# Gate and up projections by seven block products in more blocks, with merged joins, in a three-layer transformer kernel on one Trainium2 core

## The reference, cut to what matters

```python
D_FF = FFN_HIDDEN = 2816
# feed-forward of the first block (layer 0 of the kernel)
gate = jnp.einsum('bsd,df->bsf', h2, w_gate[layer])
up = jnp.einsum('bsd,df->bsf', h2, w_up[layer])
x = x + jnp.einsum('bsf,fd->bsd', jax.nn.silu(gate) * up, w_down[layer])

# feed-forward of the second block, twice (layers 1 and 2 of the kernel)
def conv_ffn(h, w_up, conv_w, conv_b, w_down):
    u = h @ w_up                                   # 1024 -> 2 * 2816
    c = lax.conv_general_dilated(u, conv_w[:, None, :], window_strides=(1,),
        padding=[(CONV_WIDTH - 1, 0)], ...) + conv_b   # 3 taps over the tokens, per channel
    g, val = jnp.split(c, 2, axis=-1)
    return (jax.nn.silu(g) * val) @ w_down
```

## Time and profile before

| | |
|---|---|
| median of 3 runs | 1713.58 us (1713.24 to 1714.19) |
| the profiled execution | 1712.91 us, its span 1711.1 us |
| PE busy in the span | 1700.8 us |
| DVE busy | 1278.1 us |
| ACT busy | 864.3 us |
| POOL busy | 361.6 us |

### The profile page before, as it was taken

One profiled execution on the slowest core, in us unless ns is written; L12 is line 12 of the kernel. 1 busy time (PEld: TensorE's weight loads), 2 busy tenths in 40 slices (PEclk: granted clock), 3 DMA queues, 4 the chain that ended last, 5 costly groups with the idle time before them and its releaser, 6 DMA issues.

```text
span 1711.1 us, 24883 instructions
## 1 busy us (share of the span) xinstructions
PE 1700.8 (99%) x9596; PEld 1476.2 (86%) x9596; DVE 1278.1 (75%) x1968; ACT 864.3 (51%) x1530; POOL 361.6 (21%) x264
## 2 busy tenths in 40 slices
PE   9999999999999999999999999999999999999998
PEld 8888888998998888888888988889898888898897
DVE  5789656897696846695979966755889687996575
ACT  5554533443354646554545533547877454454354
POOL 2003204442325011102144202022110213520200
PEclk9999999999999999999999999999999999999999
DMA  5212333334222221213233341323111234334122
GB/s 173 74 62 72 99 99 124 99 99 146 77 75 87 62 82 57 73 51 98 88 134 111 99 123 50 90 74 93 40 50 50 87 95 127 99 99 136 62 87 74
DMA packets 125196, 152.90 MB, mean 89 GB/s; under 512 B 7526, under 2 KB 96904, under 8 KB 125080
## 3 DMA queue, kind: packets, MB, share of 16 engines
q1 hardware_dynamic: 124776, 150.99, 27.9%
q10 hardware_dynamic: 304, 0.33, 0.1%
HBM read 148.61 MB, written 2.10 MB: 88 GB/s over the span
## 4 chain that ended last, share of the span: by engine, by line
PE 94%; DVE 4%; POOL 1%; issue 1%; ACT 1%; DVEq 0%; ACTq 0%; POOLq 0%
PE bk L2422 23%; PE bk L2424 23%; PE bk L2423 23%; PE bk L2464 5%; PE bk L2466 5%; PE bk L2465 5%; PE bk L2427 4%; PE bk L2569 2%; DVE FS L2624 1%; POOL FS L3011 1%; PE bk L2603 1%; PE bk L2530 1%; PE bk L2602 1%; DVE WL L2636 1%; PE bk L2557 1%
## 5 line engine op out<-in xcount | busy, mean ns | idle before, releaser
L2422 PE MATMUL bk<-R,WH 128*128 128x512 f32 (+1 forms) x1394 | 521.2, 374 | 0.9 <-DVE WL L2636 0.7
L2424 PE MATMUL bk<-R,WL 128*128 128x512 f32 (+1 forms) x1394 | 515.0, 369 | 0.0
L2423 PE MATMUL bk<-R,WH 128*128 128x512 f32 (+1 forms) x1394 | 514.8, 369 | 0.0
L2636 DVE TENSOR_TENSOR WL<-RAW,WH 128x1024 fp32r<-128x1024 f32 (+5 forms) x198 | 248.2, 1255 | 153.5 <-ACT WH L2861 152.3
L2861 ACT ACTIVATE WH<-RAW 128x1024 fp32r<-128x1024 f32 (+5 forms) x198 | 202.8, 1026 | 213.8 <-PE bk L2424 152.5
L2422 PEld LDWEIGHTS bk<-R,WH 128*128 128x128 f32 x1394 | 263.0, 189 | 45.3 <-DVE WL L2636 2.1
L2424 PEld LDWEIGHTS bk<-R,WL 128*128 128x128 f32 x1394 | 262.8, 189 | 44.9
L2423 PEld LDWEIGHTS bk<-R,WH 128*128 128x128 f32 x1394 | 263.2, 189 | 41.0
L3007 POOL TENSOR_TENSOR OVER<-TOK 128x1024 f32<-128x1024 f32 x28 | 76.3, 2725 | 382.0 <-DVE WL L2633 216.4
L2464 PE MATMUL bk<-WH,R 128*128 128x512 f32 (+4 forms) x394 | 144.7, 367 | 0.0
L2466 PE MATMUL bk<-WL,R 128*128 128x512 f32 (+4 forms) x394 | 139.3, 353 | 0.0
(11 more groups left out here) (235 smaller groups left out, 3251.8 us busy)
## 6 DMA issues: line engine op xcount, KB each, us to landing
RAW<-in_ffn_w_down_dram SPq DMA_DIRECT2D x44, 512.0 KB, 3.9
RAW<-in_ffn_w_up_dram SPq DMA_DIRECT2D x64, 256.0 KB, 3.0
TOK<-in_ffn_w_up_dram SPq DMA_DIRECT2D x14, 1024.0 KB, 5.1
RAW<-in_ffn_w_up_dram SPq DMA_DIRECT2D x28, 512.0 KB, 3.6
RAW<-in_w_down_dram SPq DMA_DIRECT2D x22, 512.0 KB, 3.6
RAW<-in_da_w_qkv_dram SPq DMA_DIRECT2D x32, 256.0 KB, 3.0
TOK<-in_w_gate_dram SPq DMA_DIRECT2D x7, 1024.0 KB, 5.4
TOK<-in_w_up_dram SPq DMA_DIRECT2D x7, 1024.0 KB, 5.0
```

The costliest lines, as they stand in the source:

```text
L2422: e.matmul(dst, lh, rh, start=start, stop=False)
L2423: e.matmul(dst, lh, rl, start=False, stop=False)
L2424: return e.matmul(dst, ll, rh, start=False, stop=stop)
L2636: e.tensor_tensor(low, sides(st.n, raw_home(st.n)), high.bitcast(F32), ALU.subtract).then_inc(on["wlo_dve"], 1)
```

## The change

- `SEVENS`: layers 1 and 2 use units for gate *and* up of blocks 4 to 10 (7 to 14 units each). Layer 0 adds block 3 (14 to 16 units), for which its parts become 3, 4 and 4 blocks (`BLOCKS`).
- The joins of a unit are four instructions instead of seven: two products that are joined alike share one bank (`o` is the column where a product begins), and a join takes both halves or writes both results. DVE does three of 512 columns and one of 256; ACT has one more copy. A unit holds five banks instead of seven.
- `Combined` takes two `FS` slots instead of four, with `PART` for the rest, gets a margin for free slots and another rank in the planner. Planning costs of `join` follow its width.

```diff
-PARTS = (range(0, 4), range(4, 8), range(8, 11))
-SEVENS = ({fb: (0, 2) for fb in range(4, 11)}, {fb: (0,) for fb in range(4, 11)}, {fb: (0,) for fb in range(4, 11)})
+THIRDS = (range(0, 4), range(4, 8), range(8, 11))
+BLOCKS = ((range(0, 3), range(3, 7), range(7, 11)), THIRDS, THIRDS)
+SEVENS = ({fb: (0, 2) for fb in range(3, 11)}, {fb: (0, 2) for fb in range(4, 11)}, {fb: (0, 2) for fb in range(4, 11)})
...
+EARLY = -2
+MARGIN = (3, 5, 5)
+RANKS = (1.5, 0.5)
...
-        if kind == "max":
+        if kind in ("max", "join"):
...
-                for kp in range(4):
-                    spawn(self.make(kp), 0.5)
+                N.uses += 4
+                self.makers = [spawn(self.make(kp), RANKS[0]) for kp in range(4)]
...
-                while kp and self.own[kp - 1] is None:
+                while kp and (self.own[kp - 1] is None or ("s4", kp - 1) not in self.of):
...
-                yield from N.use()
-                while len(fsl.fr) < 5:
-                    yield None
-                e, o, p, q = slots = [fsl.get() for _ in range(4)]
-                E, O, A, B = (FS[:, s.i, 0:S] for s in slots)
+                while N.spread is None:
+                    yield None
+                while len(fsl.fr) < self.margin:
+                    yield None
+                e, o = fsl.get(), fsl.get()
+                E, O = (FS[:, s.i, 0:S] for s in (e, o))
+                A, B = PART
...
-                    fsl.put(s, lo, w4.pool)
+                    if n < 2:
+                        fsl.put((e, o)[n], lo, w4.pool)
+                    else:
+                        part_free[n - 2] = [lo, w4.pool]
...
-            def product(n, half, name):
-                b = yield from bank("gemm")
-                st = yield step("piece", n=n, half=half, xs=X.operand(name), bank=b.i, after=counts([w_low[n].dve, X.ready, b.free]))
+            def product(n, half, name, b=None, o=0):
+                if b is None:
+                    b = yield from bank("gemm")
+                st = yield step("piece", n=n, half=half, xs=X.operand(name), bank=b.i, o=o, after=counts([w_low[n].dve, X.ready, b.free]))
                 if half or n == n2:
                     w_used[n] = st.pe
                 return b, st.pe
 
...
-            spawn(top_left(b, done), 0)
+            spawn(first(), 0)
+            b2, _ = yield from product(n1, 1, "a12")
...
-            b6, done6 = yield from product(n4, 0, "s2")
+            _, done6 = yield from product(n4, 0, "s2", b2, 256)
 
+                while q.first is None or len(fsl.fr) < 2:
+                    yield None
+                l, r = sorted((fsl.get(), fsl.get()), key=lambda s: s.i)
+                right = FS[:, r.i, 0:S]
+                st = yield step("join", dst=FS[:, l.i:r.i + 1:r.i - l.i, 0:256], src=halves_of(b2), x=one.unsqueeze(1).to_broadcast([P, 2, 256]),
+                                op=ALU.add, after=counts([done6, q.first, l.free, r.free]))
+                put_bank(b2, st.dve)
+                part_free[u % 2] = [st.dve]
+                third = yield step("join", dst=right[:, 256:S], src=BK[b7.i][:, 0:256], x=right[:, 0:256], op=ALU.add, after=counts([done7, st.dve]))
+                put_bank(b7, third.dve)
+                copied = yield step("keep", dst=FS[:, l.i, 256:S], src=right[:, 256:S], after=counts([third.dve, l.free]))
+                st = yield step("join", dst=right.rearrange("p (x c) -> p x c", x=2), src=BK[b5.i][:, 0:256].unsqueeze(1).to_broadcast([P, 2, 256]),
+                                x=right.rearrange("p (x c) -> p x c", x=2), op=ALU.subtract, after=counts([done5, third.dve, copied.act]))
+                put_bank(b5, st.dve)
+                q.low, q.both = [copied.act, st.dve], (l, r)
 
             spawn(middle(), 0)
...
+            b4, _ = yield from product(n4, 1, "a22")
+            _, done3 = yield from product(n2, 0, "s4", b4, 256)
+            X.over(done3)
+
+            def outer():
+                while q.both is None:
+                    yield None
+                l, r = q.both
+                at_l = FS[:, l.i, 256:S]
+                both = bass.AP(at_l.tensor, at_l.offset, [at_l.ap[0], [FW * (r.i - l.i) - 256, 2], [1, 256]])
+                st = yield step("join", dst=both, src=halves_of(b4), x=both, op=ALU.add, after=counts([done3, q.low]))
+                put_bank(b4, st.dve)
+                spawn(ev(0, l, st.dve), 0)
+                spawn(ev(1, r, st.dve), 0)
+
+            spawn(outer(), 0)
+
+        def halves_of(b):
+            return BK[b.i][:, :].rearrange("p (x c) -> p x c", x=2)
...
-                    if zone and part == 0 and fb == PARTS[0][-2]:
-                        held = Combined(N, counts(ptfree), counts(kfree[4 + 4 * NSK:]))
+                    if zone and part == 0 and fb == parts[0][EARLY]:
+                        part_free[0], part_free[1] = counts(tok_users), counts(tok_users)
+                        held = Combined(N, counts(ptfree), counts(kfree[4 + 4 * NSK:]), MARGIN[layer])
...
+                    for s in X.makers:
+                        s.rank = (RANKS[1], s.rank[1])
```

More of the change, by code:

```diff
@@ L502, in plan_ffn @@
                 zones[layer] = [len(chunks), len(chunks), len(units)]
-            for fb in PARTS[part]:
+            parts = BLOCKS[layer]
+            for fb in parts[part]:
                 sevenfold = SEVENS[layer].get(fb, ())
@@ L534, in build @@
         plan_rows(w_out, 512, 4)
-        for part in range(len(PARTS)):
+        for part in range(len(BLOCKS[0])):
             plan_ffn(part, ((w_gate, 0), (w_up, 0)), w_down)
@@ L546, in build @@
         plan_last_rows(da_o, 768)
-        for part in range(len(PARTS)):
+        for part in range(len(BLOCKS[1])):
             plan_ffn(part, ((up2[0], 0), (up2[0], 2816)), dn2[0])
@@ L1700, in seven @@
             q = Group()
-            q.first = q.second = q.third = q.left = q.right = q.y = None
-            one, two = PART[u % 2][:, 0:256], PART[u % 2][:, 256:S]
+            q.first = q.low = q.both = None
+            one = PART[u % 2][:, 0:256]
             def split(n):
@@ L1715, in product @@
                 return b, st.pe
-            def join(dst, b, done, x, op, *after):
-                st = yield step("join", dst=dst, bank=b.i, x=x, op=op, after=counts([done, *after]))
-                return st.dve
             while len(X.of) < 32:
@@ L1723, in seven, with first @@
             yield from split(n1)
-            b, done = yield from product(n1, 0, "a11")
-            def first(b, done):
-                st = yield step("keep", dst=one, bank=b.i, after=counts([done, part_free[u % 2]]))
-                put_bank(b, st.act)
+            b1, done1 = yield from product(n1, 0, "a11")
+            def first():
+                st = yield step("keep", dst=one, src=BK[b1.i][:, 0:256], after=counts([done1, part_free[u % 2]]))
+                put_bank(b1, st.act)
                 q.first = st.act
-            spawn(first(b, done), 0)
-            b, done = yield from product(n1, 1, "a12")
-            def top_left(b, done):
-                while q.first is None:
-                    yield None
-                s = yield from fslot()
-                q.top = yield from join(FS[:, s.i, 0:256], b, done, one, ALU.add, q.first, s.free)
-                put_bank(b, q.top)
-                q.left = s
-            spawn(top_left(b, done), 0)
+            spawn(first(), 0)
+            b2, _ = yield from product(n1, 1, "a12")
             yield from split(n3)
@@ L1764, in seven @@
-            spawn(middle(), 0)
-            b, done = yield from product(n4, 1, "a22")
-            def bottom_left(b, done):
-                while q.right is None:
-                    yield None
-                low = yield from join(FS[:, q.left.i, 256:S], b, done, one, ALU.add, q.third)
-                put_bank(b, low)
-                part_free[u % 2] = [low]
-                yield from ev(0, q.left, low)
-            spawn(bottom_left(b, done), 0)
-            yield from split(n2)
-            b, done = yield from product(n2, 0, "s4")
@@ L2864, in scalar_program @@
                         w.wait_ge(*done)
-                    e.activation(st.dst, BK[st.bank][:, 0:256], ACT.Copy).then_inc(on["keep_act"], 1)
+                    e.activation(st.dst, st.src, ACT.Copy).then_inc(on["keep_act"], 1)
                 elif k == "hi":
```

62 lines of the change are left out of this document (22 added, 40 removed).

## The result

| | before | after |
|---|---|---|
| median | 1713.88 us (1713.24 to 1714.27, 4 runs) | 1752.98 us (1751.67 to 1754.33, 4 runs) |
| the profiled execution, its span | 1712.91, 1711.1 us | 1751.67, 1749.9 us |

The ratio is 1.0231, with a 95% interval of 1.0218 to 1.0243: the kernel is 2.3% slower. The forecast of 1741 us had the direction and most of the size; the time lies in its range, 12 us above the number.

What follows compares the result with a forecast made beforehand. PE bounded the kernel before; with added taps and waits for POOL, DVE would bound layers 1 and 2: 2 x (10.3 + 3.3) + 2 = +29.2, less 1.7 in layer 0, +27.5, so 1741 us; range 1718 to 1766.

Steps and rivals of the forecast that it cites:

- The change of bound: In layers 1 and 2's parts with units, DVE's load instead of PE's work sets the length; chance 0.68.
- PE's waits: In layers 1 and 2, PE idles for low weights some 13 us per part of 8 units, 5 per part of 6.
- What POOL takes from DVE: DVE instructions with two SBUF operands wait for POOL's sums: 3.5 us per unit, read in layer 0.
- the turn: DVE's waits for POOL per unit above which the changed kernel is slower: about 2.3 us.
- Taps at 0.66 and joins at 0.60: DVE's start-to-start costs: 0.66 us per tap, also from SBUF, and 0.60 per join of 512 columns.
- The units' part of 94.2 us: Layers 1 and 2, part of 8 units (blocks 4 to 7): 94.2 us instead of 83.9, +10.3.
- The down projections at 0.5 us each (0 to 3): Down projections behind the parts with units in layers 1 and 2 begin late: 0.5 us per part, +2 for four.
- The parts of 6 units at 66.2 us: Layers 1 and 2, last part with units: 66.2 us instead of 62.9, +3.3.
- Layer 0 at -1.7 us: Block 3's added units save PE 1.7 us in layer 0; earlier combinations cost 0, bound 3.

Runs made afterwards that it cites:

- run with blocks 4, 8 and 9: The changed kernel, but in layers 1 and 2 up is a unit only in blocks 4, 8 and 9: 1718.41 us against 1713.5, ratio 1.0031.
- run with one filling matmul: The changed kernel with one more matmul of 256 columns before each product of a unit in layers 1 and 2: 1754.18 us against 1713.61, 1.0238.

## Why the prediction was right, and which terms were off

*The change of bound* held. DVE is busy for 99% of the parts of 8 units; PE waits there for low weights of `OVER` and `TOK`, and has no other cause of its waits inside them of any size. The runs without sums and with shortened taps show both halves of the reason: without POOL's sums the same change gains 10.7 us, without the taps it is at zero.

*PE's waits* were set at some 13 us in each part of 8 units and 5 in each of 6. They are 9.2 and 10.3, and 4.2 and 3.0: the rest of PE's lost time is in its slower matmuls, which count as busy.

*What POOL takes from DVE* held in size. From 925 to 1014 us DVE spends 20.3 us of 89 beyond the start-to-start times of its instructions, while POOL is busy for 36.1 us with the sums of six to seven units: 3.0 to 3.4 us per unit, where 3.5 were read in layer 0. The run without sums agrees: 97.25 - 72.96 = 24.3 us in 8 units, 3.0 each. The Trainium skill (SBUF — State Buffer, Who interferes with whom) calls the port pair that GpSimd and such a DVE instruction share an exclusive lock; the trace agrees for single instructions (3.12 instead of 1.21 us), but the cost per unit was not POOL's 5.4 us (2.42 + 2.98), since joins run beside a sum. The prediction sets the turn at about 2.3 us per unit; with its own terms it is 2.1 (27.5 over 20 units is 1.4 less than 3.5), which changes nothing here.

*Taps at 0.66 and joins at 0.60* held as start-to-start times: the four taps from SBUF at 1121.45 take 2.65 us until the next instruction starts, 0.66 each, and joined pairs of 512 columns take 0.68 us each, as forecast. A tap beside a sum takes 1.77 us (1008.68).

*The units' part of 94.2 us* was 1.2 and 1.6 us short. The sum lets the last weights decide, ready at 1008.75 in layer 1, and adds the last product: 1010.2, or 94.5 us after the start. But the chunk before them, ready at 1006.77, has 24 matmuls of its own to come first. With 36 x 0.120 that is 1011.1 at the full clock, or 95.4 us; in layer 2 it is 95.8.

*The down projections at 0.5 us each (0 to 3)* is the term that failed. "Their own weights stand a few instructions behind the last of the units'": those few are four taps and a join, 4.3 us, and PE needs the weights at once, while only the last block's activations can wait until the third quarter. From the 1011.1 at which PE could have been done it is 3.1 us to 1014.2, and 3.1 again in layer 2, in place of 0.5. (In layer 1 PE's lower clock hides 2 of them: its last product really ends at 1013.2.) In the parts of 6 units it is nothing, since the weights stand ahead of the taps there, ready at 1121.53, and PE's units end at 1124.4. Together with the term above, the parts of 8 units came out 9.0 us longer than 2 x 94.2.

*The parts of 6 units at 66.2 us* came out at 66.5 and 65.5. Some of that is luck: layer 1's holds 1.4 us of lower clock that the sum didn't have.

*The end of a layer* was left out of the sum: the stretch from the last unit to the end of the span is 45.6 us instead of 42.7, with a wait of 1.61 us for the last result. 2.9 us. The run with blocks 4, 8 and 9 shows that this can be 7 us.

*Layer 0 at -1.7 us* was half right: the first unit of layer 1 begins 0.5 us earlier. The units of block 3 start with a wait of 0.68 us for a combination (288.84 us), which was set at zero with a bound of 3. By itself the layer's change, with the merged joins, is worth -1.0 us, within 0.2%.

*The clock* wasn't in the prediction at all. It costs 1.3 to 2.5 us after a long wait, but in the parts of 8 units the kernel doesn't pay it, since DVE sets their end. The part of 6 units of layer 1 gets longer by it: the last 36 matmuls, from 1118.65, take 5.75 us to 1124.40 instead of 36 x 0.120 = 4.3, so 1.4 us. The layer doesn't, as far as the run with one filling matmul shows, which lost at `R` what it gained there.

The span: -0.5 to the first unit of layer 1, +14.6 and +15.0 in the parts of 8 units, +3.6 and +2.6 in those of 6, +0.4 in their down projections, +0.3 from there to layer 2, +2.9 at the end make 38.9 of 38.8 measured; 27.5 were forecast. Against the forecast that is 9.0 - 2.0 us for the parts of 8 units with the down projections, 2.9 for the end and 1.2 for layer 0; the rest is small.

## What to carry to other kernels

When PE is busy for 99% and the next engine for 75%, look in each stretch at how long before PE's need the other engine's last operand is ready. In layer 0's part of 8 units, which the changed parts came to resemble, that slack was 0.2 us, and the work added to DVE came out almost in full: 28 taps x 0.66 = 18.5 us, less 1.3 for the joins, made 98.5 us of 81.0. Count an engine's instructions at what they take beside the neighbour that holds them up, not at their price when it is quiet. When a piece is moved ahead in a queue, look at everything it now stands in front of: the low weights gained 1.4 us where they were late and lost 0.88 where they weren't. And replacing fewer gemms (5 units in 4 blocks and 4 in 3) kept a gain: 1.6 us, and 2.5 with layer 0's.

## What the runs showed of the hardware

TensorE's clock fell after waits that looked harmless. After 3.60 us of waiting the granted clock was 0.50 (1.2 GHz) for the next 27 matmuls, at 0.213 us from start to start instead of 0.120, and then 1.00 (2.4 GHz); after the wait of 0.64 us at 1136.11 it stayed at 1.00. The length of the wait alone doesn't tell. In the changed kernel the clock fell after 2.16 us (at 964.37; 0.59 as the mean of 964 to 968) and, from the twelfth matmul on, after 1.78 (at 1686.81; 0.74 as the mean to 1690). It stayed at 1.00 after 3.17 and 3.29 us in the kernel with one filling matmul (1561.58 and 1585.17), and after 1.76 in the one with the weights moved (1685.47). That is why PE's busy time in the parts of 8 units is 88.3 and 87.3 us and not 80.6.

Instructions on 8 columns that read two operands from SBUF are not free beside POOL: four of them took 0.63 us in one place and 1.67 in another.
